# Block 0's mixing issued inside its input projection, in a one-core decoder step with gathered experts

## The chip, the cores and the metric

The kernel runs on one core of one Trainium2 chip. The metric is the device time of one execution in microseconds; the time shown is the median of three runs. The engines are named PE (TensorE), DVE (VectorE), ACT (ScalarE), POOL (GpSimd) and SP (SyncE, which here only issues DMAs). All data are fp32.

## The reference

One step of a one-layer decoder for 1024 prompt tokens (eight blocks of 128) and 8 sample tokens. Per token:

```python
qr, kr, vr, gr, qs, ks, vs = split(rms_norm(x) @ w_in)      # 1024 x 2816
qr, kr = rotate(qr), rotate(kr) * 128 ** -0.5
o_ret  = (qr @ kr.T * decay_mask) @ vr + (qr @ state) * q_decay        # 4 heads; state carried over blocks
o_swa  = softmax_with_sink(qs @ [k_prev_block, ks].T / 8) @ [v_prev_block, vs]   # 8 query, 2 kv heads
h = x + concat(norm(o_ret) * silu(gr), o_swa) @ w_out
xn = rms_norm(h)
# PEER: 8 heads, two sets of 128 sub-keys, top 16 of each, top 16 of their 256 sums
s  = (xn @ peer_w_q) . sub_keys
idx, gates = top16, softmax(top16)                         # 128 experts per token
y = rms_norm(h + sum_k gelu(peer_u[idx_k] . xn) * gates_k * peer_v[idx_k])
```

For each block of 128 tokens the kernel must fetch 128 x 128 rows of 8 KB (`peer_u` and `peer_v` side by side), a gigabyte over all eight blocks.

## The kernel before

**Stages.** First the tokens of block 0 are projected: eight chunks of 352 columns of w_in (`project_first`, copied out of PSUM and scaled by the token's root in `first_out`). Then block 0 is mixed (`mixing`: rotation, retention, two groups of sliding-window attention), goes through w_out (`picking`, 16 matmuls of 128x512 into two banks, 32 records in the trace), is normalised, gets its scores against the sub-keys (`picking`, n = 0 to 3; n = 0 and 1 make the first half, 2 and 3 the second), and DVE ranks and chooses experts, half by half (`picks`: `rank_halves`, `choose`, `number`). From then on eight blocks run one after the other, 128 units each. In a unit POOL gathers one row per token into a ring of eight slots (`fetch`), DVE takes its dot product (`expert_dot`), ScalarE makes a diagonal of the gated activation (`weigh`), PE adds the weighted row into PSUM (`add_pair`, for two units). Beside the units of block b the mixing, scores and choice of block b+1 are done, the projections of the later blocks (the late pieces: 176 columns of w_in for one block of tokens, `project_late`, `late_out`, `store_late`) and the step of the 8 samples.

**The key weights.** The scores need `peer_w_q` multiplied by the sub-keys (`keyw`). It is made on the chip, in 32 items (`key_weights`, 16 loads wqT, two halves each: four matmuls of 128x128 into one half of `acc` on PE, one copy on ScalarE). An item must wait for the copy of the one two before it.

**What sets the order.** Each engine runs its own program in order. Within it, steps are generators that yield the tick at which their next part is due; `advance` runs all parts that are due. In a tick the parts of the front (`mixing`, `picking`) come first, then the key weights. Ahead of the first unit PE runs ticks 0 to 127, DVE and ScalarE 0 to 103. `PICK_AT` = 47 is the tick of w_out, so `at + 23` in `picking` is tick 70. `key_tick` says at which tick each key item is done, on PE and on ScalarE. All orders are fixed when the program is built; an engine that waits holds up everything behind it.

**The first block around the change.** PE does all eight chunks, waits for all their copies, then starts `mixing`, with key items between its parts: 16 before w_out, 8 behind it, 8 behind the first half's scores. The second half's scores wait for all 32. DVE makes the gains of three blocks' tokens at tick 42, and between ticks 63 and 66 it sums the squares of the later tokens' x (`count`), as they arrive; ScalarE takes their root (`tok_root`) at tick 70 and copies the first half's scores at tick 73. The second score copy is at tick 84, the first half's exponentials (`best_exp`) at tick 98. After its ticks PE does the late pieces 0 to 7, ScalarE copies them, and only then begins with its units (`begin`).

**SP's queue.** SP issues all loads and stores in one order: chunks of w_in (a buffer of three), constants, sub-keys, xT of blocks 1 to 3, four wqT loads, w_out (once chunk 6 of 8 is done), eight more wqT, gains, three late weights, residual, the rest of wqT, x of tokens for `count`, four more late weights (`RESTING`), then the stores of the late pieces 0 to 7, with the move of the first picks (`move_picks(0, 0)`, from half of the partitions to the other half) behind the store of piece 3. POOL's first fetch needs the moved picks; its fifth also needs late piece 6 and all the counts, because its slots are in use by the resting weights and x.

**Between blocks.** The dot products use x in two tiles, `xlo` and `xhi`, whose halves come from x2 directly (same partitions) and from two PE banks, into which PE has swapped them (`x2_swapped`). In `take_over` DVE copies all four halves (lines 1665 to 1668) once the last dot of the block before is done.

## Time and profile before

| | us |
|---|---|
| median of three runs | 3030.5 (3027.26 to 3035.45) |
| profiled execution | 3028.92 |
| its span | 3027.1 |
| PE, DVE, ACT, POOL busy | 2264.8, 2038.7, 1021.5, 1185.0 |
| mean granted TensorE clock | 0.858 |

The page cuts the span into 40 slices of 75.7 us; a digit is a tenth of busy time (9 is 90% or more), GB/s is what the DMA engines moved.

```profile
DVE  2474547775578655887558865787568765886865
ACT  2322522334233343422433353233433353233322
POOL 0022333433344333433443444444444444444442
DMA  8579999999999999999999999999999999999997
GB/s 329 198 292 397 401 421 421 420 416 423 420 419 400 415 423 421 421 364 393 420 421 421 420 416 421 410 416 412 420 419 419 409 409 421 420 411 395 421 422 323
```

The first two to three slices are the stage that the change touches most: there POOL hasn't begun, and the DMA strip isn't full. From slice 4 on the DMA engines are full in all slices but the last, which no compute engine is.

### The profile page before, as it was taken

How to read it: one execution, taken by the hardware profiler on the slowest of the kernel's cores; microseconds unless marked ns; L12 is line 12 of the kernel's file. 1: busy time of each engine (PE TensorE's matmuls, PEld its weight loads, DVE VectorE, ACT ScalarE, POOL GpSimd, SP SyncE). 2: the span in 40 equal slices, each digit the busy share in tenths (PEclk: the TensorE clock that was granted, in tenths of full speed). 3: DMA queues.
4: the chain of work that ended last, by engine and by line, in shares of the span. 5: the costliest groups of instructions: out<-in, count | busy, mean ns of one | idle time of the engine just before them, and what ended most of it. 6: DMA issues, size and time to landing. Idle time of an engine off the chain costs nothing.

```text
span 3027.1 us, 29088 instructions
## 1 busy us (share of the span) xinstructions
PE 2264.8 (75%) x8810; PEld 961.7 (32%) x8810; DVE 2038.7 (67%) x4942; ACT 1021.5 (34%) x3215; POOL 1185.0 (39%) x1052
## 2 busy tenths in 40 slices
PE   7889969887798868777686567766785668678564
PEld 6567613553245522232221132212221122111111
DVE  2474547775578655887558865787568765886865
ACT  2322522334233343422433353233433353233322
POOL 0022333433344333433443444444444444444442
PEclk9999989997899988966798888968898788888777
DMA  8579999999999999999999999999999999999997
GB/s 329 198 292 397 401 421 421 420 416 423 420 419 400 415 423 421 421 364 393 420 421 421 420 416 421 410 416 412 420 419 419 409 409 421 420 411 395 421 422 323
DMA packets 195454, 1213.93 MB, mean 401 GB/s; under 512 B 25496, under 2 KB 44480, under 8 KB 62048
## 3 DMA queue, kind: packets, MB, share of 16 engines
q0 software_dynamic: 148608, 1082.20, 86.5%
q1 hardware_dynamic: 46688, 129.87, 11.1%
q8 instruction: 69, 1.13, 0.1%
q14 instruction: 89, 0.73, 0.1%
HBM read 1192.28 MB, written 20.23 MB: 401 GB/s over the span
## 4 chain that ended last, share of the span: by engine, by line
DMA 39%; PE 31%; DVE 16%; issue 6%; ACT 4%; POOL 3%; SPq 1%; POOLq 0%; DVEq 0%; ACTq 0%
DMA ring<-in_peer_uv,idxg 35%; PE ps L936 14%; DVE ring L1675 8%; PE ps L677 5%; PE ps L898 5%; POOL ring L602 3%; ACT ring L1000 2%; PE ps L879 2%; DMA wo<-in_w_in 2%; DVE columns L1582 1%; DVE columns L1576 1%; PE ps L694 1%; DVE columns L1586 1%; DVE columns L1525 1%; DVE columns L1518 1%
## 5 line engine op out<-in xcount | busy, mean ns | idle before, releaser
L602 POOL DMA_INDIRECT ring<-in_peer_uv,idxg x1024 | 1169.7, 1142 | 1623.7 <-PE ps L936 1389.2
L936 PE MATMUL ps<-ring 128*64 128x512 f32 x4096 | 1245.9, 739 | 652.1 <-ACT ring L1000 651.6
L1675 DVE SCALAR_TENSOR_TENSOR ring<-ring,xlo 128x1024 f32<-128x1024 f32 x512 | 626.8, 1224 | 432.4 <-DMA ring<-in_peer_uv,idxg 417.5
L1675 DVE SCALAR_TENSOR_TENSOR ring<-ring,xhi 128x1024 f32<-128x1024 f32 x512 | 626.5, 1224 | 350.6 <-DMA ring<-in_peer_uv,idxg 342.1
L936 PEld LDWEIGHTS ps<-ring 128*64 128x64 f32 x4096 | 289.5, 158 | 1441.5 <-ACT ring L1000 981.8
L1181 ACT ACTIVATE small<-small 128x2 f32<-128x2 f32 x512 | 103.9, 203 | 1684.4 <-DVE ring L1675 1655.1
L677 PE MATMUL ps<-wo 128*128 128x176 f32 x1728 | 291.6, 325 | 30.2 <-DMA wo<-in_w_in 12.9
L1000 ACT ACTIVATE ring<-gdiag,small 128x64 f32<-128x64 f32 x1024 | 300.3, 340 | 16.8
L677 PEld LDWEIGHTS ps<-wo 128*128 128x128 f32 x1728 | 269.7, 197 | 91.7 <-issue 72.7
L1000 ACT ACTIVATE gdiag<-fold,gateg 128x64 f32<-128x64 f32 x1024 | 292.8, 333 | 1.5
L898 PE MATMUL ps<-keyw,work 128*128 128x512 f32 (+1 forms) x576 | 278.9, 620 | 1.1 <-ACT work L1000 1.1
L898 PEld LDWEIGHTS ps<-keyw,work 128*128 128x128 f32 (+1 forms) x576 | 97.8, 183 | 184.1 <-issue 182.7
L1525 DVE FIND_INDEX8 columns<-columns 128x8 uint32<-128x128 f32 (+3 forms) x432 | 135.0, 328 | 0.0
L879 PE MATMUL ps<-wo,work 128*128 128x512 f32 x224 | 110.5, 627 | 0.0
L1518 DVE MAX8 columns<-columns 128x8 f32<-128x128 f32 (+3 forms) x432 | 109.4, 321 | 1.5 <-ACT columns L1000 1.0
L1181 ACT ACT_TABLE_LOAD x64 | 82.1, 1283 | 1.1
L611 POOL COPY idxg<-stage 128x64 uint32<-128x64 uint32 x16 | 7.3, 459 | 179.4 <-DMA stage<-moving 179.3
L1533 DVE MATCH_REPLACE8 columns<-columns 128x128 f32<-128x128 f32 (+3 forms) x216 | 66.9, 319 | 0.0
L879 PEld LDWEIGHTS ps<-wo,work 128*128 128x128 f32 x224 | 40.5, 196 | 73.1 <-issue 73.1
L1582 DVE TENSOR_TENSOR columns<-columns 128x256 f32<-128x256 f32 (+1 forms) x144 | 51.4, 417 | 0.1
L1000 ACT ACTIVATE wo<-ps,small 128x176 f32<-128x176 f32 (+2 forms) x73 | 30.8, 421 | 51.6 <-PE ps L677 46.1
L1576 DVE TENSOR_TENSOR columns<-columns,small 128x1024 f32<-128x1024 f32 (+1 forms) x36 | 44.0, 1221 | 0.7
(201 smaller groups left out, 1538.3 us busy)
## 6 DMA issues: line engine op xcount, KB each, us to landing
wo<-in_w_in SPq DMA_DIRECT2D x44, 704.0 KB
ring<-in_peer_uv,idxg POOLq DMA_INDIRECT x1024
wo<-in_w_out SPq DMA_DIRECT2D x4, 4096.0 KB, 16.9
ring<-in_w_in SPq DMA_DIRECT2D x7, 1408.0 KB, 8.2
ring<-in_wqT SPq DMA_DIRECT2D x16, 512.0 KB, 4.3
columns<-proj_scratch SPq DMA_DIRECT2D x7, 896.0 KB
proj_scratch<-wo SPq DMA_DIRECT2D x70, 88.0 KB
h<-in_x_prompt SPq DMA_DIRECT2D x9, 512.0 KB, 8.1
```

What stands on the lines that cost most here:

```text
L602: nc.gpsimd.indirect_dma_start(row[r], None, A["peer_uv"], bass.IndirectOffsetOnAxis(ap=experts, axis=0)).then_inc(ld_row[r], 16)
L677: mm = nc.tensor.matmul(o, tokens_T(n, k), w[:, k, :], start=(k == 0), stop=(k == KC - 1))
L879: mm = nc.tensor.matmul(F[2 + n][0:rows, :], lhsT, weights[:, k, n * 512:(n + 1) * 512], start=(k == 0), stop=(k == KC - 1))
L898: mm = nc.tensor.matmul(F[n][0:rows, :], xT[:, k * P:k * P + rows], keyw[:, k, n * 512:(n + 1) * 512], start=(k == 0), stop=(k == KC - 1))
L936: mm = nc.tensor.matmul(acc[side * HP:(side + 1) * HP, n * 512:(n + 1) * 512], row_u[r][:, 0:HP], row_v[r][:, n * 512:(n + 1) * 512], star ...
L1000: return nc.scalar.activation(o, i, ACT.Copy, **kw_)
L1181: me.did(nc.scalar.activation(gel[:, r:r + 2], dot[:, r:r + 2], ACT.Gelu))
L1518: me.did(nc.vector.max(v16(j)[:, r8 * 8:r8 * 8 + 8], rowsof(j)))
L1525: me.did(nc.vector.max_index(i16(j)[:, r8 * 8:r8 * 8 + 8], v16(j)[:, r8 * 8:r8 * 8 + 8], rowsof(j)))
L1576: me.did(tt(one, abf[0:rows, c * HALF:(c + 1) * HALF].rearrange("p (n a) -> p n a", a=1) .to_broadcast([rows, HALF, TK]), iot, ALU.is_equal))
L1582: me.did(tt(o3, o3, i4[:, hh, c, :].rearrange("p (a k) -> p a k", a=1) .to_broadcast([rows, TK, TK]), ALU.mult))
L1675: ins = stt(row_u[r], row_u[r], 1.0, (xlo, xhi)[unit % 2][:], ALU.mult, ALU.mult, accum_out=dot[:, r:r + 1])
```

## The change

- The eight chunks are projected in another order (`CHUNK_ORDER`): the columns of Q and K first, then gate, sliding Q, K and V, then retention V and the rest of the gate. They use three banks instead of four.
- PE's part of block 0's mixing (`mixing_first`) is issued between the chunks. DVE does both sliding groups ahead of `retained` (scaling and state update, formerly inline). ScalarE copies chunks 4 to 7 between its own steps; both groups of exponentials come ahead of silu and of the root. The functions `silu`, `exponentials`, `weights_out`, `turn_weights`, `weigh_values`, `turn_mixed` and `retained` hold lines that stood inline before.
- The key items get a table of ticks: two items inside the mixing, two behind it, two ahead of w_out, seven behind it, three between the first two score groups, sixteen behind the first half's scores. Score group n waits for 8(n+1) items. ScalarE copies items at tick 27 or later.
- On ScalarE the later tokens' root stands directly behind the first score copy, not ahead of it; DVE's gains move from tick 42 to 63.
- SP's order changes: w_out right behind two wqT loads, x of tokens 1 and 2 and the residual ahead, x 3 to 8 behind wqT 9, the first picks' move ahead of all late stores.
- In every block the two swapped halves are copied by ScalarE (`take_halves`, at the head of `begin`), and DVE waits for them; PE waits for both before it overwrites the banks.

```diff
+CHUNK_ORDER = (0, 1, 2, 5, 6, 7, 3, 4)
...
+KEY_TICKS = [22, 22, 27, 27, 46, 46, 60, 60, 62, 62, 62, 62, 65, 69, 69, 69] + [73] * NHC + [END]
...
+def key_copy_tick(done):
+
+    return max(KEY_TICKS[done], 27)
...
+        FIRST_BANKS = [ps[:, 0, :], ps[:, 1, :], F[5]]
+        FIRST_HEADS = (F[4], F[5])
...
+                of = 2 * CHUNK_ORDER[c]
                 sp.dma_start(wbuf[c % 3].rearrange("p (a f) -> p a f", a=2),
-                             A["w_in"][2 * c:2 * c + 2].rearrange("a p f -> p a f")).then_inc(ld_w[c % 3], 16)
+                             A["w_in"][of:of + 2].rearrange("a p f -> p a f")).then_inc(ld_w[c % 3], 16)
...
             sp.dma_start(skT, A["sub_keysT"]).then_inc(ld_skT, 16)
+            for n in range(2):
+                load_wqT(n)
+            sp.dma_start(wo_first.rearrange("p k n -> p (k n)"), A["w_out"]).then_inc(ld_wo_first, 16)
+            for n in range(2, 4):
+                load_wqT(n)
             sp.dma_start(xT_early.rearrange("p (n f) -> p n f", n=3), A["xT"][1:4].rearrange("n p f -> p n f")
                          ).then_inc(ld_xT_early, 16)
-            for n in range(4):
-                load_wqT(n)
-            sp.wait_ge(pj_mm, NCH - 2)
-            sp.dma_start(wo_first.rearrange("p k n -> p (k n)"), A["w_out"]).then_inc(ld_wo_first, 16)
-            for n in range(4, 12):
-                load_wqT(n)
             for dst, src in ((g2b, A["norm2_g"]), (gfb, A["final_g"])):
                 sp.dma_start(dst[:], rows_of(src, D)).then_inc(ld_gains, 16)
+            for n in range(1, 3):
+                load_x(n)
+            load_wqT(4)
+            load_residual(0)
+            for n in range(5, 10):
+                load_wqT(n)
+            for n in range(3, TILES):
+                load_x(n)
+            for n in range(10, 12):
+                load_wqT(n)
             for l in range(3):
                 load_late(l)
-            load_residual(0)
-            sp.dma_start(proj_d[P:SEQ, 0:ROPE], A["c_rope"][P:SEQ, :]).then_inc(st_rope, 16)
             for n in range(12, NHC):
                 load_wqT(n)
-            for n in range(1, 5):
-                load_x(n)
             for l in RESTING:
                 load_late(l)
-            for n in range(5, TILES):
-                load_x(n)
+            sp.dma_start(proj_d[P:SEQ, 0:ROPE], A["c_rope"][P:SEQ, :]).then_inc(st_rope, 16)
+            move_picks(0, 0)
             for q in range(AHEAD):
                 l = PIECES[q][0]
                 if l not in RESTING and q == LAST_OF[l]:
                     load_late(TURNS[TURNS.index(l) + 3])
                 store_late(q)
-                if q == 3:
-                    move_picks(0, 0)
...
-                if c >= BANKS:
-                    pe.wait_ge(pj_out, c - (BANKS - 1))
+                if c >= len(FIRST_BANKS):
+                    pe.wait_ge(pj_out, c - len(FIRST_BANKS) + 1)
+                bank = FIRST_BANKS[c % len(FIRST_BANKS)]
...
+            def mixing_first():
+                for c in range(4):
+                    project_first(c)
+                pe.wait_ge(ld_first, 32)
+                pe.wait_ge(roped, 1)
+                for j in range(8):
+                    t = T(FF(0, 2)[:, j * P:(j + 1) * P], proj[:, j * P:(j + 1) * P])
+                t.then_inc(qkT_mm, 1)
+                project_first(4)
+                pe.wait_ge(qkT_out, 1)
+                for hh in range(RH):
+                    mm = nc.tensor.matmul(F[0][:, hh * P:(hh + 1) * P], xT[:, 512 + hh * P:512 + (hh + 1) * P],
+                                          xT[:, hh * P:(hh + 1) * P], start=True, stop=True)
+                mm.then_inc(st_mm, 1)
+                project_first(5)
+                pe.wait_ge(pj_out, 6)
+                for j in range(4):
+                    T(F[2][:, j * P:(j + 1) * P], proj[:, C_QS + j * P:C_QS + (j + 1) * P])
+                T(F[3][:, 0:P], proj[:, C_KS:C_VS]).then_inc(qsT_mm, 1)
+                for hh in range(RH):
+                    nc.tensor.matmul(F[1][:, hh * P:(hh + 1) * P], xT[:, hh * P:(hh + 1) * P], state[:, hh, :],
+                                     start=True, stop=True)
+                project_first(6)
+                pe.wait_ge(qsT_out, 1)
+                sliding(0)
+                project_first(7)
+                pe.wait_ge(sw_nmax, 1)
+                sliding(1)
+                pe.wait_ge(sw_exp, 1)
+                turn_weights(0, FIRST_HEADS)
+                pe.wait_ge(pj_out, NCH)
+                pe.wait_ge(stm_ready, 1)
+                for hh in range(RH):
+                    mm = nc.tensor.matmul(F[0][:, hh * P:(hh + 1) * P], x2[:, hh * P:(hh + 1) * P],
+                                          proj[:, C_V + hh * P:C_V + (hh + 1) * P], start=True, stop=True)
+                mm.then_inc(ret_mm, 1)
+                pe.wait_ge(kd_ready, 1)
+                pe.wait_ge(pT_out, 1)
+                for hh in range(RH):
+                    mm = nc.tensor.matmul(F[4][:, hh * P:(hh + 1) * P], x2[:, 512 + hh * P:512 + (hh + 1) * P],
+                                          proj[:, C_V + hh * P:C_V + (hh + 1) * P], start=True, stop=True)
+                mm.then_inc(kv_mm, 1)
+                mixed[0] = 1
+                yield 24
+                pe.wait_ge(ret_taken, 1)
+                weigh_values(0)
+                pe.wait_ge(sw_exp, 2)
+                turn_weights(1, heads_of(1))
+                yield 26
+                pe.wait_ge(pT_out, 2)
+                weigh_values(1).then_inc(sw_o, 1)
+                yield 41
+                turn_mixed(0)
...
+            def turn_weights(j, banks):
+                for q in range(8):
+                    t = T(banks[q // 4][:, q % 4 * P:(q % 4 + 1) * P], swp[j][:, q * P:(q + 1) * P])
+                t.then_inc(pT_mm, 1)
+
+            def weigh_values(j):
+                for i in range(GRP):
+                    o = F[0][:, (j * GRP + i) * SD:(j * GRP + i + 1) * SD]
+                    pT = swp[j][:, i * 256:(i + 1) * 256]
+                    nc.tensor.matmul(o, pT[:, 0:P], vprev[:, j * SD:(j + 1) * SD], start=True, stop=False)
+                    mm = nc.tensor.matmul(o, pT[:, P:2 * P], proj[:, C_VS + j * SD:C_VS + (j + 1) * SD],
+                                          start=False, stop=True)
+                return mm
...
             def mixing(b):
                 yield 13
                 if b:
                     pe.wait_ge(x2_taken, b)
+                    pe.wait_ge(halves_taken, b)
...
-                    if b == 0 and n >= 2:
-                        pe.wait_ge(keyw_out, (2 * NHC if n == 3 else 24) + 2)
+                    if b == 0:
+                        pe.wait_ge(keyw_out, 8 * (n + 1) + 2)
...
-            for c in range(NCH):
-                project_first(c)
-            pe.wait_ge(ld_first, 32)
-            pe.wait_ge(pj_out, NCH)
...
-                copy(proj[:, c * CW:(c + 1) * CW], F[c % BANKS][:, 0:CW], scale=tok_root[:, 0:1]).then_inc(pj_out, 1)
+                of = CHUNK_ORDER[c] * CW
+                copy(proj[:, of:of + CW], FIRST_BANKS[c % len(FIRST_BANKS)][:, 0:CW], scale=tok_root[:, 0:1]
+                     ).then_inc(pj_out, 1)
...
+            def weights_out(b, j, banks):
+
+                act.wait_ge(pT_mm, b * 2 + (j + 1))
+                for n in range(2):
+                    ins = copy(swp[j][:, n * 512:(n + 1) * 512], banks[n])
+                ins.then_inc(pT_out, 1)
...
                 copy(xT, FF(0, 2)).then_inc(qkT_out, 1)
+                if b == 0:
+                    first_out(4)
+                    first_out(5)
...
-                yield 24
-                act.wait_ge(ret_mm, b + 1)
-                nc.scalar.activation(x2[:, 0:512], proj[:, C_G:C_G + 512], ACT.Silu).then_inc(silu_ready, 1)
...
+                if b == 0:
+                    first_out(6)
+                    exponentials(0, 0)
+                    first_out(7)
+                    weights_out(0, 0, FIRST_HEADS)
+                    yield 22
+                    exponentials(0, 1)
+                    silu(0)
+                    yield 25
+                    weights_out(0, 1, heads_of(1))
+                    yield 26
+                    root(rstd)
+                else:
+                    yield 24
+                    silu(b)
+                    for j in range(KVH):
+                        yield 26 + 6 * j
+                        exponentials(b, j)
+                        if j == 0:
+                            yield 28
+                            root(rstd)
+                        yield 31 + 6 * j
+                        weights_out(b, j, heads_of(j))
...
-                if b == 0:
-                    yield at + 23
-                    root(tok_root[:, 1:TILES])
                 for half in range(2):
                     yield at + 29 + half * 16 if b else at + 26 + half * 11
                     act.wait_ge(sc_mm, b * 4 + (2 * half + 2))
                     copy(proj[0:rows, half * D:(half + 1) * D], FF(2 * half, 2 + 2 * half)[0:rows, :]
                          ).then_inc(sc_out, 1)
+                    if b == 0 and half == 0:
+                        root(tok_root[:, 1:TILES])
...
+            def take_halves(b):
+
+                if b:
+                    act.wait_ge(dots, b * PAIRS)
+                    act.nop(nofuse=True)
+                act.wait_ge(x2_swapped, b + 1)
+                copy(xlo[HP:P, :], FF(0, 2)[HP:P, :])
+                copy(xhi[0:HP, :], FF(0, 2)[0:HP, :]).then_inc(halves_taken, 1)
+
             def begin(b):
+                take_halves(b)
...
-            for c in range(NCH):
+            for c in range(4):
...
-                yield 42
+                yield 63
...
-                    yield 63 + n // 3
+                    yield 64 + n // 4
...
                 tt(x2[:, 0:512], F[0], dmaskT[:].rearrange("p h m -> p (h m)"), ALU.mult).then_inc(stm_ready, 1)
+                o = xT[:, 0:512]
+                if first:
+                    yield from sliding(b, 0, mask)
+                    yield from sliding(b, 1, mask)
...
+                retained(b, o)
...
-                                      mixr_ready, 26, sliding(b, 1, mask))
+                                      mixr_ready, 26, () if first else sliding(b, 1, mask))
...
-                me.did(nc.vector.tensor_copy(xlo[HP:P, :], FF(0, 2)[HP:P, :]))
-                me.did(nc.vector.tensor_copy(xhi[0:HP, :], FF(0, 2)[0:HP, :]))
                 me.sync()
                 tell(x2_taken)
+                v.wait_ge(halves_taken, b + 1)
+                v.nop(nofuse=True)
```

## Rows read from the trace of the kernel before

**Rows 1.** Windows; columns: stretch us, length, busy time per engine, PEclk, DMA share, GB/s.

```profile
0.00:179.60 179.60, 152.78 (x740) 111.08 (x741) 72.04 (x209) 48.08 (x90) 1.63 (x7) 0.96 0.65 238
144.00:163.00 19.00, 19.00 (x71) 9.64 (x70) 17.97 (x82) 4.30 (x7) 0.00 (x0) 1.00 0.00 1
230.00:260.00 30.00, 30.00 (x174) 24.18 (x173) 12.22 (x30) 10.82 (x31) 6.40 (x6) 0.96 0.96 371
1330.00:1340.00 10.00, 8.85 (x26) 3.07 (x27) 9.16 (x20) 4.28 (x16) 4.35 (x3) 0.74 0.32 106
2334.00:2342.00 8.00, 4.63 (x14) 0.83 (x10) 7.47 (x17) 1.81 (x7) 3.54 (x3) 0.79 1.02 424
```

**Rows 2.** Timeline: start us, us, engine, line, operation [idle before <-releaser]; the first fetch.

```profile
173.63 0.50 SPq L465 DMA_DIRECT2D stage<-moving  x1
178.11 1.10 POOL L602 DMA_INDIRECT ring<-in_peer_uv,idxg  x1 [0.97 <-POOL idxg L611]
```

**Rows 3.** Timeline, block 0's projection and mixing.

```profile
25.50 23.93 PE L650 MATMUL ps<-ring,wo 128*128 128x352 f32 x80 [1.43 <-DMA ring<-in_w_in]
61.77 1.99 PE L862 MATMUL ps<-kTb,columns 64*128 64x256 f32 x8
63.80 1.29 DVE L1487 SCALAR_TENSOR_TENSOR h<-ps,ring 128x512 f32<-128x512 f32 x2 [1.34 <-PE ps L862]
66.77 0.17 DVE L1498 TENSOR_SCALAR small<-small 128x4 f32<-128x4 f32 x1
70.72 1.28 ACT L1110 ACT_TABLE_LOAD   x1
72.02 0.51 ACT L1110 ACTIVATE h<-h,small 128x256 f32<-128x256 f32 x1
74.00 0.19 ACT L1113 ACTIVATE small<-small 128x4 f32<-128x4 f32 x1
88.43 0.69 DVE L1477 TENSOR_TENSOR columns<-ps,small 128x512 f32<-128x512 f32 x1 [5.38 <-PE ps L850]
91.44 14.00 PE L879 MATMUL ps<-ring,work 128*128 128x512 f32 x32 [1.11 <-ACT work L1000]
```

**Rows 4.** Timeline, from the output projection to the first ranking.

```profile
105.28 7.67 PE L694 MATMUL ps<-ring 128*128 128x128 f32 x64
111.69 1.28 ACT L1009 ACT_TABLE_LOAD   x1
116.97 15.49 PE L898 MATMUL ps<-keyw,work 128*128 128x512 f32 x32 [1.11 <-ACT work L1000]
138.01 0.21 ACT L1009 ACTIVATE small<-small 128x8 f32<-128x8 f32 x1 [21.10 <-DVE small L1268]
139.24 1.65 DVE L1518 MAX8 columns<-columns 128x8 f32<-128x128 f32 x8 [0.78 <-ACT columns L1000]
```

**Rows 5.** Timeline, the end of the first half's choice.

```profile
168.45 0.22 DVE L1594 TENSOR_REDUCE small<-gates 128x4 f32<-128x64 f32 x1
169.67 0.19 DVE L1613 TENSOR_TENSOR moving<-gates,small 64x32 f32<-64x32 f32 x1
```

**Rows 6.** Timeline, the late pieces and the first rows.

```profile
162.98 7.43 PE L677 MATMUL ps<-wo 128*128 128x176 f32 x48
182.38 0.41 ACT L1000 ACTIVATE stg_more<-ps,small 128x176 f32<-128x176 f32 x1 [1.98 <-PE ps L677]
183.87 1.23 DVE L1675 SCALAR_TENSOR_TENSOR ring<-ring,xlo 128x1024 f32<-128x1024 f32 x1 [10.06 <-DMA ring<-in_peer_uv,idxg]
194.39 0.94 POOL L602 DMA_INDIRECT ring<-in_peer_uv,idxg  x1 [6.01 <-PE ps L936]
```

**Rows 7.** Timeline at two block boundaries.

```profile
1324.79 1.23 DVE L1667 COPY xlo<-ps 64x1024 f32<-64x1024 f32 x1
1330.70 0.20 ACT L1000 ACTIVATE wo<-ps 128x32 f32<-128x32 f32 x1 [6.59 <-PE ps L761]
2341.72 1.02 ACT L1000 ACTIVATE work<-ps 128x1024 f32<-128x1024 f32 x1 [2.65 <-PE ps L936]
```

More of the change, by code:

```diff
@@ L788, in mixing, with turn_mixed @@
+            def turn_mixed(b):
+                pe.wait_ge(mixr_ready, b + 1)
+                pe.wait_ge(mixs_ready, b + 1)
+                for k in range(KC):
+                    t = T(FF(0, 2)[:, k * P:(k + 1) * P], proj[:, C_MIX + k * P:C_MIX + (k + 1) * P])
+                t.then_inc(mixT_mm, 1)
             def mixing(b):
@@ L913, in front @@
             def front(b):
-                yield from mixing(b)
+                yield from mixing(b) if b else mixing_first()
                 yield from picking(b, P, PICK_AT)
@@ L1042, in key_weights @@
                              ).then_inc(keyw_out, 1)
-                        yield key_tick(2 * n + half + 1)
+                        yield key_copy_tick(2 * n + half + 1)
             def sample():
```

84 lines of the change are left out of this document (32 added, 52 removed).

## The prediction

> **What bounds the kernel now.** I read the page's strip of slices first: DMA at 9 tenths in nearly every slice, except 5 and 7 tenths in the second and third. The windows then say how full. In a plain stretch the DMA share is 1.02 at 424 GB/s, across a block boundary too [rows 1], while over the first 179.6 us it is 0.65 at 238 GB/s, with a window of 19 us in which nothing at all is moved [rows 1]. So from the first gathered expert row on the kernel is a stream of 1,214 MB that the DMA engines set, and only two things can shorten it: idle DMA time ahead of the first row, and the few places behind it where the stream runs dry (371 GB/s from 230 to 260 us; 106 GB/s from 1330 to 1340, where the sample step is) [rows 1]. The first row is asked for at 178.11, 4.5 us behind the move of the picks at 173.63 [rows 2]. The timeline up to there is the whole argument.
>
> The profiled execution took 3028.9 us, its span 3027.1 with 1.8 around it; the median of the three timed runs is 3030.5, 1.6 above. I work out the saving against the profile and take it off the median.
>
> **Part 1, mixing inside the projection.** Before, five chunks run on PE without a gap, 23.93 us from 25.50, 4.79 each [rows 3], and mixing follows from 50 until W_out starts at 91.44 [rows 3]. In the new order PE does, from 25.50:
> - five chunks 23.9, and between them eight transposes 1.0, the retention scores 1.0, five transposes and the state product 1.7 with 0.6 for the copy of the chunk before them, and both sliding groups 2.0 each [rows 3]. (An item of eight records 128x128 is 7.67/8 = 0.96 [rows 4].) Sum 32.2: PE is through at 57.7. The rotation of Q and K lies beside the fourth chunk, as before. First maxima: 3.2 us from the matmul's end to nmax (63.76 to 66.94 [rows 3]), beside the last chunk, ready at 54.4.
> - ScalarE's first exponentials, table load included, 70.72 to 74.19 = 3.5 [rows 3]: 54.4 to 57.9. Eight transposes to 59.1, retention 60.1, the copy out of PSUM (two of 0.55) to 60.3, state product to 61.5.
> - DVE: scale, four state steps, sum: 0.7 + 0.9 + 0.7 and handoffs, ret_taken at 64.0. PE weighs values 1.9, turns the second group 1.0: 66.9. ScalarE copies it out by 68.1 and, with a table load, gives the root at 69.6. DVE: reciprocal and two 128x512 products of 0.69 [rows 3]: 71.3; the sliding product: 72.7. The second exponentials (61.1 to 63.3) and silu (to 65.3) are ready before they are asked for.
> - eight transposes to 73.8, then key items 4 and 5 (2.0), which cover the copy of 1.0: W_out starts at 75.8, **15.6 earlier**. Its weights, asked for at 49, are there by about 64 at the rate of the windows. Bounds of this step: 0 (every handoff costs what it saves) to 17 (items 4 and 5 fall away).
>
> **Part 2, from W_out to the first ranking.** Before: W_out ends at 105.4, first score starts at 116.97, scores end at 132.46, but ScalarE is held from before until 138.01 in the root of the later tokens (idle 21.10 behind DVE, which waits for x), so ranking starts at 139.24 [rows 4]. After:
> - W_out ends at 89.8; DVE's norm reaches its root at 92.5. Before, ScalarE came to it only at 112.99, behind six key copies and a table load of 1.28 [rows 4]; now only items 6 and 7 are ahead (92.4), and since nothing but copies follows rstd's root, no load is needed: 92.8. x2 at 94.3. PE has items 6 to 11 meanwhile, but 10 and 11 each wait for a copy two items back that stands behind that root: 95.6. Transposes 1.0, copy 1.0 with handoffs: scores start at 97.8, 8.0 behind W_out where it was 11.6.
> - Items 13 to 15 now stand between the two score groups: 3 x 0.96, and 0.9 for the last copy: +3.8. Two groups of 7.0 [rows 3]: scores end at **115.6**, 16.8 earlier. (Before they took 15.49 instead of 14.0, the first 3 us at the low clock [rows 4]; I leave up to 1.5 for that.)
> - The copy goes first now (116.6), the root behind it takes 0.2. Its sums: x 3 is behind wqT 9 in SP's queue, that is behind item 11 at 95.6, and x 5 to 8 behind the counts. Landing in 7 us each round, with the three gains of 3.5 us ahead of the counts, DVE is done at about 112 to 115; I take it as covered, by as little as 2 us. If a round takes 10 us, that is 4 us on the path. Ranking starts at 117.3, **21.9 earlier**.
>
> **Part 3, to the first row.** The choice takes from 139.24 to 169.86 [rows 4, 5], 30.6. It reads the exponentials 29.2 behind its start [rows 4, 5], so at 146.5. Those stand behind the second score copy: 115.6 + 16 items 15.4 + two groups 14.0 = 145.0 [rows 3, 4], copy 1.0, load and exponential 1.5: 147.6. So a new wait of 1.1 appears; topk at 149.0. The move was 3.8 behind it, since it stood behind the store of piece 3 [rows 2, 5]; it now stands ahead of the stores: 149.1, first fetch at **153.6 instead of 178.1** [rows 2].
>
> **What of it counts.** Three late pieces take 7.43, one 2.4 [rows 6]. They start at 147.7 instead of 162.98. Two more gates open with them: the fifth fetch waits for piece 6 (164.6), and the first dot waits for ScalarE, which copies all eight pieces (167.5 instead of 182.8 [rows 6]) and then the swapped halves. Price of these two copies: the nearest rows are 1.02 for 128x1024 on ScalarE and 1.23 for the same half on DVE [rows 7]; I take 1.02, so 169.6; both ends differ by 0.4. The first dot goes from 183.87 to 169.6, and so does the ninth fetch, from 194.39 to 180.1 [rows 6]: **14.3 by this chain**. The stream itself starts 24.2 earlier but has more to do behind its start: three weight loads of 704 KB and five stores of 88 KB, 2.6 MB, 6.1 us at 424 GB/s: **18.1 by the stream**. Eight rows of 1.05 MB (19.8 us) and these loads keep it full from 155 to about 184, past the ninth fetch. Where it runs dry (230 to 260 [rows 1]) the chain counts, elsewhere the stream: I take 16.
>
> **Part 4, the halves at each boundary.** DVE loses two copies of 1.23 and waits for ScalarE's two of 1.02, which there start 0.8 behind the last dot: the first dot comes about 1.2 earlier, and ScalarE still has its gate diagonals done before it may copy the sum (2341.72, idle 2.65 ahead of it [rows 7]). The stream is full there (1.02 [rows 1]): 0, between -1 and +1. At the boundary by the sample step ScalarE is stuck until 1330.70 behind PE's sample matmuls [rows 7]; the first dot there, before at 1327.4 (1324.79 and DVE's last two copies of 1.23 [rows 7]), will wait to 1332.9 (1330.90 and two of 1.02), while the stream is dry anyway [rows 1]. That costs 0 to 5, I take 2.
>
> Sum: 16 - 2 = 14. 3030.5 - 14 = **3016.5** (3014.9 profiled).
>
> A rule that bears on the order of ScalarE's functions: in rows 3 the exponential starts 0.02 after the table load of 1.28 ended, so a switch costs 1.3 here. The Trainium skill, ScalarE: Activation LUTs, section on what ACT_TABLE_LOAD costs, gives 1283 ns and a drain of some 1380 more for each switch. On that rule the two switches that block 0's chain loses would be worth 2.8 us more and the saving nearer 17; by this rule, the trace agrees on the load and shows no drain.
>
> **Rivals.**
> - A, the new waits eat part: 17 handoffs between PE, ScalarE and DVE are lined up in block 0's mixing, each of which I priced at 0.1 to 0.2. If each is 0.5 more (rows show waits of 1.11 from a ScalarE copy of 1.0, so little, but also 1.34 in front of DVE [rows 3]), 8.5 us go, and the saving is 5.5: 3025. For it: many small steps in series. Against: the same handoffs stand in the old timeline at these prices.
> - B, the stream decides throughout and the sample boundary is free: saving 18.1, 3012.4. For it: DMA share 1.02. Against: the dry windows [rows 1].
> - C, slower: at every boundary the first dot waits for ScalarE as by the sample step, 1332.9 against 1327.4, 5.5 us. It decides as soon as the ring's eight rows (19.8 us of stream) are drained by then. Seven boundaries: 38.5 - 16 = 22.5 slower, 3053. Against: ScalarE is at most 1 us behind the last dot at a boundary without samples, and the stream is full.
> - D, the change doesn't bring the first row forward as it says: the key items behind the first scores have wqT 12 to 15 as their loads, each of which may take 5.8 us from its issue. If such a load takes 10, each of the four pairs waits some 4 us: 16 us later second scores, exponentials and pieces: all of it gone, 3031. For it: three loads of 704 KB now stand ahead of wqT 12. Against: they are moved by then (5 us).
>
> **How the numbers follow.** A difference under 0.3% (9.1 us) can't be told from none here. Forecast 0.62 (its own range 3011 to 3022), A 0.18, B 0.12, C 0.03, D 0.05. Faster: 0.59 + 0.12 + 0.04 = 0.75; same: 0.03 + 0.14 + 0.03 = 0.20; slower 0.05. The range goes from B's 3012 less 3 for part 1's and the clock's bounds, 3009, to A's 3025 and one more: 3026.
>
> **What would show it.** W_out at 75 to 77 in the timeline (part 1); scores' end at 115 to 118 and ranking within 2 us of it, with the root of the later tokens behind the copy (part 2; if DVE waits there, the x loads were late); first fetch at 153 to 156; a DVE wait on the first dot that ends with ScalarE's copy, at 169 to 171, and the ninth fetch at 180 to 182; DMA share near 1 from 156; the dry window at the sample step 0 to 5 us longer, all other boundaries as before. Wrong if W_out starts later than 82, if the fifth fetch leaves the DMA engines idle for more than 3 us, or if boundaries other than the sample's run dry.

## The result, and the profile after

The changed kernel takes 3003.6 us (median of six runs, 3000.6 to 3008.5) where the kernel before takes 3032.9 beside it: a ratio of 0.9912, 95% interval 0.9901 to 0.9924, so 27 us less (23 to 30; the two medians are 29.2 apart). Forecast were 3016.5 and a range of 3009 to 3026: the direction was right, the size half of what came, and the time lies below the range. The profiled execution took 3001.6, its span is 2999.7, 27.4 less than before; its mean granted clock is 0.869. All times of single events below are from one execution each.

From the page, the strip of slices (75.0 us each, a digit is a tenth of the DMA engines' time):

```profile
DMA  8599999999999999989999999999999999999998
GB/s 326 208 397 417 407 420 421 414 419 423 419 417 412 417 419 421 415 363 402 421 421 421 416 411 421 421 417 401 420 421 420 408 416 421 414 414 395 416 421 333
```

The gain is in the third and fourth slice, 397 and 417 GB/s where there were 292 and 397; from the fifth on the two strips are alike. Windows of the changed kernel (window, its length, busy us of PE, PEld, DVE, ACT, POOL, granted clock, DMA share, GB/s), which answer to [rows 1]:

```profile
0.00:152.60 152.60, 139.69 (x679) 98.98 (x680) 69.75 (x207) 44.53 (x85) 1.60 (x7) 1.00 0.72 267
150.00:160.00 10.00, 10.00 (x69) 10.00 (x69) 0.00 (x0) 1.91 (x5) 4.06 (x5) 1.00 0.94 347
180.00:190.00 10.00, 7.77 (x47) 5.92 (x46) 9.69 (x33) 3.32 (x12) 3.04 (x3) 1.00 0.99 381
210.00:220.00 10.00, 10.00 (x63) 8.42 (x62) 5.08 (x17) 4.18 (x11) 1.87 (x2) 1.00 1.02 380
230.00:260.00 30.00, 27.94 (x154) 20.74 (x153) 11.80 (x25) 6.57 (x24) 9.80 (x9) 0.94 1.02 414
1305.40:1315.40 10.00, 8.85 (x24) 2.75 (x25) 7.21 (x14) 5.14 (x12) 4.41 (x4) 0.72 0.37 116
```

Three things are to be seen. Until 1.5 us behind the first fetch 267 GB/s x 152.6 = 40.7 MB have been moved, where it was 42.7 MB; so 2.0 MB are left behind the start. The stretch from 230 to 260, which ran at 371 GB/s before, now has 414; its place is taken by two smaller dips (381 and 380). And by the sample step the DMA engines are as empty as before (116 against 106 GB/s).

The timeline of PE, from the last projection chunk but one to the late pieces (start, us, engine, line, operation):

```profile
50.89 5.00 PE L663 MATMUL ps<-ring,wo 128*128 128x352 f32 x16
57.74 1.09 PE L641 MATMUL ps<-ident,h 128*128 128x128 f32 x8
...
74.75 13.90 PE L957 MATMUL ps<-ring,work 128*128 128x512 f32 x32
88.48 5.77 PE L707 MATMUL ps<-ring 128*128 128x128 f32 x48
96.24 7.13 PE L976 MATMUL ps<-keyw,work 128*128 128x512 f32 x16 [0.22 <-ACT work L1074]
103.21 2.90 PE L707 MATMUL ps<-ring 128*128 128x128 f32 x24
106.79 7.13 PE L976 MATMUL ps<-keyw,work 128*128 128x512 f32 x16 [0.69 <-ACT keyw L1074]
113.76 13.51 PE L707 MATMUL ps<-ring 128*128 128x128 f32 x112
127.50 2.05 PE L707 MATMUL ps<-ring 128*128 128x128 f32 x16 [0.23 <-DMA ring<-in_wqT]
129.39 13.90 PE L976 MATMUL ps<-keyw,work 128*128 128x512 f32 x32
145.09 7.43 PE L690 MATMUL ps<-wo 128*128 128x176 f32 x48
```

W_out starts at 74.75 instead of 91.44 [rows 3]; the two score groups (L976) end at 113.92 instead of 132.46 [rows 4]; each takes 7.13, together 14.26 where before they took 15.49. The granted clock is 1.00 in this kernel's window from 0 to 152.6. ScalarE:

```profile
91.40 0.20 ACT L1083 ACTIVATE small<-small 128x1 f32<-128x1 f32 x1 [0.33 <-DVE small L1381]
...
113.96 1.02 ACT L1074 ACTIVATE columns<-ps 128x1024 f32<-128x1024 f32 x1 [7.22 <-PE ps L976]
114.88 0.20 ACT L1083 ACTIVATE small<-small 128x8 f32<-128x8 f32 x1
...
143.33 1.02 ACT L1074 ACTIVATE columns<-ps 128x1024 f32<-128x1024 f32 x1 [13.14 <-PE ps L976]
144.37 1.28 ACT L1255 ACT_TABLE_LOAD   x1
145.67 0.26 ACT L1255 ACTIVATE gates<-gates 128x64 f32<-128x64 f32 x1
...
164.49 0.41 ACT L1074 ACTIVATE stg_more<-ps,small 128x176 f32<-128x176 f32 x1 [1.98 <-PE ps L690]
164.92 1.02 ACT L1074 ACTIVATE xlo<-ps 64x1024 f32<-64x1024 f32 x1
165.95 1.02 ACT L1074 ACTIVATE xhi<-ps 64x1024 f32<-64x1024 f32 x1
```

The root at 91.40 needs no table load, the first score copy no longer waits for the later tokens' root (0.20 at 114.88), and the swapped halves stand behind the last late piece. DVE and POOL:

```profile
108.85 1.21 DVE L1409 SCALAR_TENSOR_TENSOR ring<-ring 8x1024 f32<-8x1024 f32 x1
115.54 1.65 DVE L1638 MAX8 columns<-columns 128x8 f32<-128x128 f32 x8 [0.22 <-DVE small L1387]
...
146.02 0.22 DVE L1714 TENSOR_REDUCE small<-gates 128x4 f32<-128x64 f32 x1 [1.29 <-ACT gates L1255]
167.07 1.23 DVE L1795 SCALAR_TENSOR_TENSOR ring<-ring,xlo 128x1024 f32<-128x1024 f32 x1 [18.20 <-issue]
```

```profile
151.13 1.09 POOL L614 DMA_INDIRECT ring<-in_peer_uv,idxg  x1 [0.97 <-POOL idxg L623]
...
162.96 0.94 POOL L614 DMA_INDIRECT ring<-in_peer_uv,idxg  x1 [7.01 <-PE ps L690]
...
177.60 0.93 POOL L614 DMA_INDIRECT ring<-in_peer_uv,idxg  x1 [9.98 <-PE ps L1014]
```

The last count of x rows is done at 110.1, ranking (L1638) starts at 115.54 (139.24 before), the first fetch at 151.13 (178.11 [rows 2]), the first dot at 167.07 (183.87) and the ninth fetch at 177.60 (194.39 [rows 6]). The first fetch came 27.0 earlier, the first dot and the ninth fetch only 16.8. The time fell by 27.

### The profile page after: what moved, and what is told of

Read it like the earlier page. It is cut to its first block, busy times and chain, and to the rows that moved or that the text cites. A ratio compares the mean times of both kernels' runs of the same rounds, so it can differ in the third digit from the quotient of the medians.

```text
span 2999.7 us, 29106 instructions
## 1 busy us (share of the span) xinstructions
PE 2236.9 (75%) x8810; PEld 946.1 (32%) x8810; DVE 2019.1 (67%) x4926; ACT 1035.0 (35%) x3229; POOL 1179.9 (39%) x1052
## 4 chain that ended last, share of the span: by engine, by line
DMA 38%; PE 32%; DVE 16%; issue 6%; ACT 4%; POOL 3%; SPq 0%; POOLq 0%; DVEq 0%; ACTq 0%
DMA ring<-in_peer_uv,idxg 36%; PE ps L1014 15%; DVE ring L1795 8%; PE ps L976 6%; PE ps L690 5%; POOL ring L614 3%; ACT ring L1074 2%; PE ps L957 1%; DMA wo<-in_w_in 1%; DVE columns L1702 1%; DVE columns L1696 1%; PE ps L663 1%; DVE columns L1645 1%; DVE columns L1706 1%; ACT small L1284 1%
## 5 line engine op out<-in xcount | busy, mean ns | idle before, releaser
L1074 ACT ACTIVATE ring<-gdiag,small 128x64 f32<-128x64 f32 x1024 | 300.3, 340 | 16.8
L976 PE MATMUL ps<-keyw,work 128*128 128x512 f32 (+1 forms) x576 | 276.7, 616 | 0.9 <-ACT keyw L1074 0.7
L976 PEld LDWEIGHTS ps<-keyw,work 128*128 128x128 f32 (+1 forms) x576 | 96.8, 182 | 182.3 <-issue 181.1
L1638 DVE MAX8 columns<-columns 128x8 f32<-128x128 f32 (+3 forms) x432 | 109.4, 323 | 0.7 <-DVE small L1387 0.2
```

Of the source, the lines that this page charges most:

```text
L976: mm = nc.tensor.matmul(F[n][0:rows, :], xT[:, k * P:k * P + rows], keyw[:, k, n * 512:(n + 1) * 512], start=(k == 0), stop=(k == KC - 1))
L1074: return nc.scalar.activation(o, i, ACT.Copy, **kw_)
L1638: me.did(nc.vector.max(v16(j)[:, r8 * 8:r8 * 8 + 8], rowsof(j)))
```

## The experiments

Two theories were set against each other. The **stream theory**: the time is set by when the stream of rows begins and by what has to be moved behind its beginning. The **chain theory**: it is set by the chain through the late pieces, the first dot and the ninth fetch, which the forecast had counted as half the answer. The table is the summary. Lead of the fetches is against the kernel before, in us. "Bytes" are those moved until 1.5 us behind the first fetch, less 42.7 MB, over 424 GB/s; "rule" is the first fetch's lead plus this. "At 200" is the lead in bytes moved until 200 us (50.8 MB before), over 424 GB/s: where "rule" and it agree, the DMA engines were as full between the first fetch and 200 us as in the kernel before. That agreement says nothing of what comes behind 200 us; the last column does.

| kernel | first fetch's lead | bytes | rule | at 200 | ninth fetch's lead | ratio to before, 95% interval |
|---|---|---|---|---|---|---|
| changed | 27.0 | -4.7 | 22.3 | 21.7 | 16.8 | 0.9912 (0.9901, 0.9924) |
| e1_halves_dve | 28.3 | -4.8 | 23.5 | 23.6 | 25.1 | 0.9915 (0.9901, 0.9929) |
| e4_halves_first | 27.6 | -4.7 | 22.8 | 22.6 | 24.4 | 0.9913 (0.9897, 0.9928) |
| e3_root_ahead | 28.2 | -4.8 | 23.5 | 23.6 | 18.1 | 0.9910 (0.9895, 0.9925) |
| e2_move_late | 17.7 | 0.0 | 17.7 | 17.0 | 16.7 | 0.9924 (0.9910, 0.9938) |
| e10_spare_bytes | 27.1 | -4.8 | 22.3 | 21.2 | 16.9 | 0.9941 (0.9928, 0.9955) |
| e11_x_late | 9.7 | -4.6 | 5.0 | 5.2 | -0.5 | 0.9964 (0.9952, 0.9976) |
| e6_x_root_only | 7.6 | -0.2 | 7.4 | 7.5 | 7.6 | 0.9972 (0.9960, 0.9984) |
| e7_no_mixing_order | 8.2 | -4.6 | 3.6 | 2.8 | 3.1 | 0.9973 (0.9965, 0.9982) |
| e5_move_only | -0.7 | -4.7 | -5.4 | -4.2 | -4.7 | 0.9992 (0.9983, 1.0001) |
| e8_halves_only | 0.8 | 0.0 | 0.8 | 0.9 | 0.3 | 0.9998 (0.9989, 1.0006) |
| e9_mixing_order_only | -0.6 | -0.1 | -0.7 | -0.5 | -0.6 | 1.0000 (0.9991, 1.0009) |

**Does the first dot bind?** Two kernels free it, in different ways.

```diff
 # e1_halves_dve: the changed kernel, take_over on VectorE, for every block
-                v.wait_ge(halves_taken, b + 1)
+                me.did(nc.vector.tensor_copy(xlo[HP:P, :], FF(0, 2)[HP:P, :]))
+                me.did(nc.vector.tensor_copy(xhi[0:HP, :], FF(0, 2)[0:HP, :]))
 # e4_halves_first: the changed kernel, ScalarE
             def begin(b):
-                take_halves(b)
+                if b:
+                    take_halves(b)
 ...
+            take_halves(0)          # ahead of the eight copies of late pieces
```

> The changed kernel with one part undone: VectorE copies the two swapped halves itself at every block start, ScalarE none. The stream theory (the time is set by when the stream of rows starts and by what has to be moved behind it; the first dot and the ninth fetch bind nothing): the first fetch stays at 151.1 us, the first dot now waits only for its row and comes near 157 instead of 167.1, the ninth fetch at 170 to 174 instead of 177.6, and the time is that of the changed kernel, 0 to 2 us less for it at the start, and within 5 us at the block start by the sample step, where the first dot should come near 1303 instead of 1308.1. The chain theory (the first dot and with it the ninth fetch set the time): the ninth fetch's 4 to 7 us are gained in full, time 4 to 7 us less.

> The changed kernel with ScalarE copying block 0's two swapped halves ahead of the eight late pieces instead of behind them. The first dot should come near 157 to 158 us instead of 167.1, the late pieces' copies 2.0 later each at most, and the ninth fetch 0 to 5 us earlier than 177.6 (it also waits for the first pair's matmuls). Stream theory: time within 0 to 2 us below the changed kernel's. Chain theory: lower by all that the ninth fetch gains, up to 5 us.

POOL in e1_halves_dve:

```profile
149.83 1.10 POOL L614 DMA_INDIRECT ring<-in_peer_uv,idxg  x1 [0.97 <-POOL idxg L623]
...
169.31 0.94 POOL L614 DMA_INDIRECT ring<-in_peer_uv,idxg  x1 [2.84 <-PE ps L1012]
```

The ninth fetch starts at 169.31 there, and at 170.03 in e4_halves_first: 8.3 and 7.6 earlier than in the changed kernel, a little more than expected; the first dot starts at 159.26 and 160.80 (expected near 157, and 157 to 158). By the sample step it starts at 1301.85 in e1_halves_dve (expected near 1303). Neither time is lower: medians 3006.0 and 3005.3 against 3003.6, with intervals that cover each other. The first dot and the ninth fetch have some 8 us of slack in the changed kernel; there the chain theory falls.

**Does the first fetch bind?**

```diff
 # e2_move_late: the changed kernel
-            move_picks(0, 0)
             for q in range(AHEAD):
                 ...
                 store_late(q)
+                if q == 3:
+                    move_picks(0, 0)
```

> The changed kernel with the first move of the picked rows put back behind the store of piece 3. First fetch some 8 us later (near 159.6 instead of 151.1), while first dot (167.1) and ninth fetch (177.6) should stay where they are within 1 us, since both wait for the late pieces' copies. Stream theory: the time grows by those 8 us (6 to 9). Chain theory: the time stays (within 1 us).

```profile
160.44 1.09 POOL L615 DMA_INDIRECT ring<-in_peer_uv,idxg  x1 [0.97 <-POOL idxg L624]
...
177.72 0.94 POOL L615 DMA_INDIRECT ring<-in_peer_uv,idxg  x1 [7.25 <-PE ps L1015]
```

Here it is the other way: the ninth fetch keeps its place (177.72), the first is 9.3 later. The profiled execution has a span of 3006.9, 7.2 more; the medians differ by 5.3, and the ratios' intervals still overlap. The sign is that of the stream theory; the size lies between the rule's 4.6 (22.3 less 17.7: the stores and weights that now go first are 2.0 MB less behind the start) and the expected 8. That these bytes would be repaid was missing in the expectation. Since the intervals overlap, this run alone doesn't settle it.

**What does a byte behind the start cost?**

```diff
 # e10_spare_bytes: the changed kernel, behind the stores of the first eight pieces
+            sp.dma_start(spare_d, x_p[0:5 * P, :]).then_inc(spare_in, 16)
```

> The changed kernel plus one copy of 2.62 MB from DRAM to DRAM (the first 640 rows of x to a place that nobody reads), issued behind the stores of the first eight late pieces. Stream theory: first fetch unchanged near 151, and the time grows by 6.2 us (2.62 MB at 424 GB/s), twice that if a copy within DRAM costs the DMA engines its bytes twice. Chain theory (the stream has slack behind the start): less than 2 us.

The first fetch stayed (151.00), the ninth too (177.47), the span is 3006.6, 6.9 more, and the median 3011.8, 8.2 more. 2.62 MB take 6.2 at 424 GB/s; the cost is nearer to that than to twice it or to the 2 of the chain theory. So the stream has no slack in which added bytes would be free. It isn't shown that bytes that are only moved, from ahead of the start to behind it, are paid in full: the changed kernel, e5, e7 and e11, which leave 2.0 MB behind, gained 4 to 8 more than their rule says.

**The parts on their own.** Each of these starts from the kernel before.

```diff
 # e5_move_only: the move ahead of the stores (e2's edit, reversed)
 # e6_x_root_only
+            for n in range(1, 3): load_x(n)        # behind the gains
 ...
+            for n in range(3, TILES): load_x(n)    # ahead of key weights 12
                     copy(proj[...], FF(...)).then_inc(sc_out, 1)
+                    if b == 0 and half == 0:
+                        root(tok_root[:, 1:TILES])
 # e7_no_mixing_order: e6 with e5 and take_halves
 # e8_halves_only: take_halves alone
```

> The kernel before with one edit: the first move of the picked rows ahead of the stores of the late pieces. First fetch some 3.8 to 4.5 us earlier (near 174 instead of 178.1), first dot (183.9) and ninth fetch (194.4) where they were. Stream theory: the time falls by 3 to 4.5 us. Chain theory: it stays.

> The kernel before with one edit: the later tokens' rows of x loaded ahead of the last key weights, and the root of the later tokens behind ScalarE's first score copy. ScalarE should copy the scores at 132.5 instead of 138.0, and ranking starts 4.5 to 5.8 us earlier than 139.2; everything behind it, first fetch, late pieces, first dot and ninth fetch, moves by as much unless the exponentials' old place behind the second score copy catches it. Both theories: time 3 to 6 us less; a rival, that the x loads delay the last key weights by their 4 MB of stream: second scores late and no gain.

> The kernel before with all of the change but the mixing order (and the key items' and projection's order with it): x and root of the later tokens early, the first move ahead of the stores, the halves on ScalarE. Stream theory: first fetch 8 to 10 us earlier (168 to 170), time 7 to 10 us less; so that 17 to 20 of the change's 27 us are left for the mixing order. Chain theory: ninth fetch only 4.5 to 5.8 earlier, time 4 to 6 less.

> The kernel before with one edit: ScalarE copies the two swapped halves at every block start. Start: first dot about 2 us later than 183.9, ninth fetch up to 2 later. At the block start by the sample step the first dot near 1332.9 instead of 1327.4. Stream theory: no change at the start, and 0 to 5 us at the sample step only if the ring has run dry by then; time within 2 us of the kernel before. The forecast's term was a loss of 2.

The x rows with the root gave 8.5 us (0.9972; 4.8 to 12.1), somewhat more than the expected 3 to 6: ranking began at 133.29, 5.95 earlier, and the first fetch came 7.6 earlier. The move gave 2.4 (the interval reaches from 5.2 to -0.3): the profiled execution started ranking at 144.47, 5.2 later than before for no edit of this kernel, so the fetch's lead has to be read from ranking, 34.4 behind it instead of 38.9; that is 4.5 earlier with 4.7 of bytes moved behind it. The expected 3 to 4.5 are not confirmed, and nothing can be told from zero. Together with the halves it is 8.2 (e7), no more than the x rows alone; there the fetch's lead of 8.2 shrinks to 3.6 by the rule, but the ratio (5.5 to 10.6) has the greater value. The halves alone changed nothing that shows (0.9998; from 3.3 less to 1.8 more).

**The mixing order on its own.** By difference it had to be worth 18.

```diff
 # e9_mixing_order_only: the changed kernel with the halves on VectorE, the move behind piece 3,
 # the root ahead of the first score copy, and
-            for n in range(1, 3):
-                load_x(n)
 ...
-            for n in range(3, TILES):
-                load_x(n)
 ...
             for l in range(3):
                 load_late(l)
+            for n in range(1, TILES):
+                load_x(n)
             for n in range(12, NHC):
 # e11_x_late: the changed kernel with this edit of the x loads alone
 # e3_root_ahead: the changed kernel with the root ahead of the first score copy alone
```

> The changed kernel with only the new order of block 0's mixing, projection and key weights left: halves on VectorE, first move behind the store of piece 3, the later tokens' root ahead of the first score copy, and all x loads behind key weights 11 (where the changed kernel has two of them before key weights 4). Additive parts: the rest of the change was worth 6.7 to 9 us on its own, so this should keep 18 to 20 of the 27: time 3010 to 3014, ranking near 121 if ScalarE waits in that root as before, near 115.5 if not. Rival, the parts cover each other (the x rows arrive early enough in the new order anyway): first fetch as in the kernel with the late move alone (160.4), time near 3006 to 3009. Rule from the nine traces so far, in both cases: the lead at 200 us is the first fetch's lead less the bytes left behind it over 424 GB/s.

> The changed kernel with one edit: all eight loads of later tokens' x rows (4 MB) behind key weights 11 and the three late projection weights, instead of two ahead of key weights 4 and six ahead of key weights 10. Theory of the covering parts (the mixing order pays only where x is early): ScalarE stands in the later tokens' root, now behind the first score copy, until VectorE has counted all rows near 129 to 130 us, the key weights' copies 14 to 31 wait behind it, the second scores end near 160, and the first fetch comes at 170 to 178: time 3022 to 3031. Rival (it was the root's place ahead of the score copy, not the rows, that took the gain): ranking at 115.5, first fetch at 151 to 155, time 3004 to 3009.

> The changed kernel with the later tokens' root on ScalarE put back ahead of the first score copy. Their sums are done on VectorE at 110.2 us, before the scores end at 113.9, so under both theories the placement itself is worth nothing now: ranking starts at 115.5 within 0.4, time within 1 us. The rival, that the placement was the gain: ranking 2 to 6 us later and the time by as much.

e9_mixing_order_only takes as long as the kernel before (1.0000; its median is 3030.7, where one side expected 3010 to 3014 and the other 3006 to 3009). ScalarE in it:

```profile
129.91 0.21 ACT L1080 ACTIVATE small<-small 128x8 f32<-128x8 f32 x1 [23.31 <-DVE small L1378]
```

It stands 23.31 us in the later tokens' root, because VectorE waits for x rows that were loaded late. W_out had ended as early as in the changed kernel (88.5). Ranking starts at 131.13, still 8.1 earlier than before, but the key items wait behind the root, the late pieces start at 162.93 (162.98 before), and the move of the picks stands behind piece 3: the first fetch comes at 178.67, and nothing is left. In e11_x_late the root is behind the first score copy, and the wait is still there (the DVE line is the first count of x rows, which ranking stands behind, too; the PE line is the key items):

```profile
117.42 1.22 DVE L1407 SCALAR_TENSOR_TENSOR xlo<-xlo 128x1024 f32<-128x1024 f32 x1 [20.85 <-DMA xlo<-in_x_prompt]
114.03 1.02 ACT L1072 ACTIVATE columns<-ps 128x1024 f32<-128x1024 f32 x1 [7.22 <-PE ps L974]
129.95 0.21 ACT L1081 ACTIVATE small<-small 128x8 f32<-128x8 f32 x1 [14.90 <-DVE small L1379]
130.79 16.06 PE L705 MATMUL ps<-ring 128*128 128x128 f32 x112 [15.02 <-ACT keyw L1072]
```

The key items behind it wait for ScalarE's copies, so PE stands still for 15.02 and its granted clock falls; windows of the same kernel:

```profile
110.00:120.00 10.00, 5.77 (x26) 3.43 (x24) 2.43 (x4) 1.02 (x1) 0.00 (x0) 0.98 0.99 391
120.00:130.00 10.00, 0.00 (x0) 0.00 (x0) 7.60 (x15) 0.05 (x1) 0.00 (x0) 0.50 0.61 209
130.00:140.00 10.00, 9.21 (x56) 9.24 (x57) 9.17 (x59) 4.72 (x9) 0.00 (x0) 0.66 0.31 104
150.00:160.00 10.00, 10.00 (x25) 4.37 (x23) 9.45 (x22) 0.00 (x0) 0.00 (x0) 1.00 0.18 64
```

From 120 to 130 PE is busy for 0.00 us, the granted clock is 0.50 (1.2 GHz), and in the ten us behind it 0.66. Ranking starts at 130.62, and POOL:

```profile
168.43 1.10 POOL L612 DMA_INDIRECT ring<-in_peer_uv,idxg  x1 [0.97 <-POOL idxg L621]
...
194.90 0.94 POOL L612 DMA_INDIRECT ring<-in_peer_uv,idxg  x1 [9.98 <-PE ps L1012]
```

This kernel also separates the theories best: its ninth fetch is 0.5 later than before [rows 6] and its first fetch 9.7 earlier. The chain theory gives no gain, the rule 5.0; measured are 7.0 by the spans and 10.9 (7.3 to 14.5) by the ratio. What was expected by the covering parts is met but for 1 us in the time (3021.1 against 3022 to 3031) and 1.6 in the first fetch (168.43 against 170 to 178). e3_root_ahead, where the x rows are early, loses nothing from the root's old place (ScalarE gives the root at 108.73, ahead of the scores' end; ranking at 114.29, 1.2 ahead of what was expected): time 3006.0, interval 0.9895 to 0.9925. So of the second part it is the rows' early arrival that counts.

By the ratios the gains hang together like this: early rows (with the root's place) alone 8.5, mixing order alone 0, mixing order with early rows but the late move 23.0 (e2), mixing order with the early move but late rows 10.9 (e11), early rows with the early move 8.2 (e7), all three 27. Besides the new order of the mixing, both the rows and the move must be ahead before it pays in full.

**What stays open.** The rule tells of the lead at 200 us within 1.2 in all twelve profiles, but of the time less well: by the ratios the changed kernel, e2, e5, e7 and e11 are 4 to 8 us better than their rule, and for these five it lies outside the interval; the others are within 4 (e10 once its 6.2 are taken off). In none is the gain smaller than the rule by more than 0.2, so here it was a lower bound. One possible reason is that each rule compares one execution with the single profile of before, and the starts of both vary by some us (e5's ranking began 5.2 late); how much that explains wasn't tried, nor was what of the dips behind 200 us hangs on the lead. No experiment beat the changed kernel.

## Why the forecast was half of what came

- **Part 1** held: W_out at 74.75 (forecast 75.8), 16.7 earlier. PE had the projection and both sliding groups behind it at 57.74, where the transposes of the weights begin, forecast 57.7.
- **Part 2** held, forecast a little too late: scores' end 113.92 (115.6), ranking 115.54 (117.3). Of the 1.7 some 1.1 are W_out's earlier start and end, 0.4 the way to the first score (7.6 behind W_out instead of 8.0), and 0.4 the items between the groups (3.4 instead of 3.8); the groups themselves took 0.3 more than the 14.0. The 1.5 left open for the low clock wasn't needed: both groups took 7.13, at a granted clock of 1.00. DVE's counts were done at 110.1 (112 to 115) and covered.
- **Part 3 to the first row** held: DVE waits 1.29 for the exponentials (forecast 1.1), first fetch 151.13 (153.6). The chain held as well: fifth fetch 162.96 (164.6), last piece copied by 164.90 (167.5), first dot 167.07 (169.6), ninth fetch 177.60 (180.1). With it the whole chain of forecast times was right within 2.6 us.
- **The step that failed** is "Where it runs dry (230 to 260) the chain counts, elsewhere the stream: I take 16." It took a figure between the chain's 14.3 and the stream's 18.1. The chain bound nothing: the ninth fetch may come 8 us earlier (e1, e4) without a gain, and 0.5 later than before with one (e11). Taking the stream alone was rival B, which had 0.12, and its 3012.4 was still 9 too high. Of the 13 us that the forecast of 14 lacks, 6.3 lie between these 16 and the measured lead of 22.3, and 2 are the sample step's term; the remaining 5 or so stay open.
- **The stream's own term was too small.** Forecast 24.2 less 6.1 = 18.1; measured 27.0 less 4.7 = 22.3, by 200 us 21.7. Of the 4.2 missing, 2.8 are the earlier first fetch (0.3 of them because the sum took 24.2 where its own 153.6 gives 24.5) and 1.4 that 2.0 MB were left behind, where I had counted 2.6.
- **The dry places were counted as a loss, and no loss shows.** The dip from 230 to 260 was argued as a place where the shorter lead of the chain holds. Behind the earlier start it became shallower (414 against 371 GB/s): the lead in bytes is 21.7 at 200 us, and by the block starts (DVE's first copy of a block's x) it is 25.0 at block 1, then 24.6, 24.6, 26.2, 26.4, 26.3, 26.6, and 27.4 at the end. That it grew is not shown to be more than chance: from 200 us to block 1 it goes from 23.6 to 26.6 in e1, but from 22.6 to 22.4 in e4 and from 23.6 to 22.9 in e3.
- **Part 4** failed at the sample step in its size. The wait that it named is there:

```profile
1305.71 0.20 ACT L1074 ACTIVATE wo<-ps 128x32 f32<-128x32 f32 x1 [6.18 <-PE ps L774]
1305.94 1.02 ACT L1074 ACTIVATE xlo<-ps 64x1024 f32<-64x1024 f32 x1
1306.97 1.02 ACT L1074 ACTIVATE xhi<-ps 64x1024 f32<-64x1024 f32 x1
```

```profile
1298.78 0.69 DVE L1785 COPY xlo<-work 64x1024 f32<-64x1024 f32 x1
1308.09 1.23 DVE L1795 SCALAR_TENSOR_TENSOR ring<-ring,xlo 128x1024 f32<-128x1024 f32 x1 [7.90 <-ACT xhi L1074]
```

  The first dot waits 7.90 for ScalarE and starts 9.3 behind DVE's first copy (1298.78); before, it started 4.1 behind it (1323.35 to 1327.41, whose third copy is in [rows 7]). It is 5.2 later, as forecast. Its price of 2 is not to be found: the block's interval (block 3's start to block 4's) is 1.7 shorter than before, not longer. Against the one profile of before it is 1.3 to 4.1 shorter with the halves on ScalarE (eight profiles) and 1.4 to 4.5 shorter with them on DVE (e1, e5, e6, e9); it varies by 3 us from execution to execution and not with the edit. Elsewhere the halves cost nothing, as forecast.
- **Rivals.** A (handoffs cost 0.5 more each) is refuted by W_out's start; C (a wait at each boundary) by e8 at 0.9998; D (key weights late) by one wait of 0.23 in front of an item. The range's low end was B less 3. It had no case in which the first fetch's whole lead counts, though the row of [rows 1] with DMA share 1.02 stood for it.

On the table loads, the row decides against the larger price: the exponential's table load begins at 144.37, 0.02 behind the copy of 1.02 that started at 143.33, and the exponential 0.02 behind the load, 1.3 for the switch as before. The Trainium skill, ScalarE: Activation LUTs, section on what ACT_TABLE_LOAD costs, adds a drain of 1380 ns to the load; by this rule the two switches would have been worth 2.8 more. No run here shows that drain, and the forecast's other steps met their times without it.

## What to carry to other kernels

In a kernel that streams at the DMA engines' limit, find the first transfer of the stream, and count as the least gain its lead less the bytes that are left behind it over the stream's rate (here 22 of the 27); of later milestones (the first use of a row, the reuse of a buffer), ask whether the DMA engines are seen to run dry in front of them: here they weren't, and these milestones had some 8 us to spare. Two edits on one serial stretch should not be priced one by one: the shorter mixing was worth nothing until the rows and the move behind it were put ahead too, and the single gains (0, 8.5, 2.4 and 0.6) are together 11.5 of the 27. And where two bounds give different answers, decide by the profile which one holds, and keep the other as a rival; a figure between them stands for neither.

## What the runs showed of the hardware

- A copy of 2.62 MB within DRAM, beside a full stream of gathered rows, cost 6.9 us by the spans (380 GB/s for bytes that are counted once) and 8.2 by the medians (320). The slices of the pages, some 75 us each, go up to 423 GB/s in the kernel before and in the changed one. The Trainium skill, DMA: Bandwidth & Descriptors, section on where 436 GB/s comes from, has 435 GB/s as the limit of the ports; the slices agree (97% of it). The same section has some 358 GB/s per core as what binds transfers between HBM and SBUF; with the one core running here, the slices stand above that.
- The start doesn't repeat well with the old order. The kernel before, e8_halves_only and e5_move_only have the same program up to the ranking, which began at 139.24, 137.14 and 144.47; with the new order PE is busy 137 of the first 150 us at a granted clock of 1.00 (before 123 of 150 at 0.95, e5_move_only 122 at 0.93), and the five profiles of kernels with that same program up to there (changed, e1, e2, e4, e10) have the ranking between 114.6 and 116.0. That the steadier start comes from the clock or from the busier PE is not shown.
